# Block products of a gated FFN in another order, with other openings, and VectorE making two low weight parts

## The reference

```python
def swiglu(x, w_gate, w_up, w_down):
    return (jax.nn.silu(x @ w_gate) * (x @ w_up)) @ w_down

x = x + 0.5 * swiglu(rmsnorm(x, ffn1_norm), ffn1_w_gate, ffn1_w_up, ffn1_w_down)
...
x = x + concat([lru_out, ssd_out]) @ w_out
x = x + 0.5 * swiglu(rmsnorm(x, ffn2_norm), ffn2_w_gate, ffn2_w_up, ffn2_w_down)
```

## Time and profile before

| | us |
|---|---|
| median of 3 runs | 2204.09 (2202.66 to 2207.38) |
| the profiled execution, its own time | 2212.14 |
| its span, first to last instruction | 2210.2 |
| TensorE busy | 2140.0 (97%) |
| VectorE, GpSimd, ScalarE busy | 1462.6, 1225.7, 593.7 |
| chain that ended last: TensorE, VectorE, VectorE's queue | 78%, 8%, 4% |

### The profile page before, as it was taken

One profiled execution on the slowest core, in us unless ns is written; L12 is line 12 of the kernel. 1 busy time (PEld: TensorE's weight loads), 2 busy tenths in 40 slices (PEclk: granted clock), 3 DMA queues, 4 the chain that ended last, 5 costly groups with the idle time before them and its releaser, 6 DMA issues.

```text
span 2210.2 us, 36672 instructions
## 1 busy us (share of the span) xinstructions
PE 2140.0 (97%) x15504; PEld 2105.7 (95%) x15504; DVE 1462.6 (66%) x1259; ACT 593.7 (27%) x856; POOL 1225.7 (55%) x825
## 2 busy tenths in 40 slices
PE   6999999988999999899999999999999999989998
PEld 5989999988999999889999999999999999989998
DVE  7797778763222567877888596787888777642215
ACT  5211101111000224577877540122100101110003
POOL 7778888872442322325352663335988888824340
PEclk8999999999999999999999999999999999989999
DMA  4122222226321322311110422132212222363222
GB/s 146 58 77 79 76 77 97 73 101 220 96 73 58 111 93 90 120 65 51 40 60 31 173 87 89 48 116 77 69 67 97 77 77 78 108 221 90 82 58 77
DMA packets 64755, 197.84 MB, mean 90 GB/s; under 512 B 9416, under 2 KB 18120, under 8 KB 64592
## 3 DMA queue, kind: packets, MB, share of 16 engines
q1 hardware_dynamic: 63440, 194.97, 26.0%
q10 hardware_dynamic: 1152, 0.52, 0.1%
HBM read 149.37 MB, written 46.26 MB: 89 GB/s over the span
## 4 chain that ended last, share of the span: by engine, by line
PE 78%; DVE 8%; DVEq 4%; ACT 3%; DMA 2%; issue 2%; POOL 1%; POOLq 1%; ACTq 0%; SPq 0%
PE banks L770 41%; PE banks L850 30%; PE banks L1117 2%; PE banks L815 2%; DMA stage<-hidden 2%; POOLq L663 1%; DVEq L1577 1%; DMA hidden<-up 1%; DVEq L1594 1%; DVE rstd L1538 1%; DVEq L1555 1%; DVE mix L1559 0%; POOL w L664 0%; DVEq L1558 0%; DVE h_lo L1640 0%
## 5 line engine op out<-in xcount | busy, mean ns | idle before, releaser
L623 POOL TENSOR_SCALAR w_hi<-w_raw 128x1024 fp32r<-128x1024 f32 (+1 forms) x93 | 106.6, 1146 | 597.2 <-PE banks L770 531.4
L625 POOL TENSOR_TENSOR w_lo<-w_raw,w_hi 128x1024 fp32r<-128x1024 f32 (+1 forms) x100 | 270.3, 2703 | 162.2 <-DVE xbc L1886 123.4
L770 PE MATMUL banks<-h_hi,w_lo 128*128 128x344 f32 x948 | 306.2, 323 | 14.4 <-DVE x L1672 14.4
L770 PE MATMUL banks<-h_lo,w_hi 128*128 128x344 f32 x948 | 304.9, 322 | 0.0
L770 PE MATMUL banks<-h_hi,w_hi 128*128 128x344 f32 x948 | 304.8, 322 | 0.0
L770 PE MATMUL banks<-u_hi,w_lo 128*128 128x344 f32 x864 | 286.4, 331 | 6.4 <-issue 6.1
L770 PE MATMUL banks<-u_hi,w_hi 128*128 128x344 f32 x864 | 276.4, 320 | 0.0
L770 PE MATMUL banks<-u_lo,w_hi 128*128 128x344 f32 x864 | 276.0, 319 | 0.0
L1672 DVE SCALAR_TENSOR_TENSOR x<-banks,x 128x1032 f32<-128x1032 f32 x42 | 51.7, 1232 | 301.3 <-PE banks L770 301.3
L1197 ACT ACTIVATE parts<-banks 128x516 f32<-128x516 f32 x80 | 47.6, 597 | 659.1 <-PE banks L850 659.1
L770 PEld LDWEIGHTS banks<-h_hi,w_lo 128*128 128x128 f32 x948 | 180.0, 190 | 15.0 <-DVE x L1672 15.0
(11 more groups left out here) (353 smaller groups left out, 5953.4 us busy)
## 6 DMA issues: line engine op xcount, KB each, us to landing
w_raw<-in_gate_up SPq DMA_DIRECT2D x46, 512.0 KB, 4.3
hidden<-up SPq DMA_DIRECT2D x44, 516.0 KB, 6.2
stage<-hidden SPq DMA_DIRECT2D x44, 516.0 KB, 3.6
raw<-in_gate_up SPq DMA_DIRECT2D x40, 512.0 KB, 4.6
w_raw<-in_w_in SPq DMA_DIRECT2D x36, 512.0 KB, 4.2
w_raw<-in_down SPq DMA_DIRECT2D x32, 512.0 KB, 3.9
x<-in_xt SPq DMA_DIRECT2D x16, 516.0 KB, 6.6
x_kept<-x SPq DMA_DIRECT2D x16, 516.0 KB, 5.1
```

The costliest lines, as they stand in the source:

```text
L623: pool.tensor_scalar(w_hi[s][:, 0:n], w_raw[s][:, 0:n], 1.0, 0.0, ALU.mult, ALU.add)
L625: pool.tensor_tensor(w_lo[s][:, 0:n], w_raw[s][:, 0:n], w_hi[s][:, 0:n].bitcast(F32), ALU.subtract).then_inc(split, 1)
L770: end = pe.matmul(out[:, c, 0:CH], w[s][:, k * P:(k + 1) * P], x[kx][:, c * CH:(c + 1) * CH], start=(first and n == 0), stop=(last and n = ...
```

## The change

1. *Order of products.* In a group now p1, p2, p6, p5, p7, p3, p4 (`STEADY`); in group 0 of a block p1, p2, p3, p6, p5, p7, p4 (`OPENING`), whose first two use neither mixes nor weight sums. Only p1 is copied by ScalarE; all others are joined by VectorE straight from PSUM, p7 twice, with one part tile in place of four. The gate or up tile 0 is multiplied by rstd before the join of p4.
2. *Plain units* are three chunks of 344 columns in three banks; copies are one operation each. VectorE reads u1 from PSUM itself, multiplying by rstd, as the last of its four multiplies. Group 0 has new waits: on the root, on that multiply (third product in the first block, second in the second), on the mixes' low parts (fourth). `norm_sum` stands at k = 6.
3. *Opening of the first block.* TensorE runs the high products of g0 and u0 (`highs`), then all low ones (`low`). VectorE makes all low x parts before the mixes, the totals of the norm (GpSimd did), and the low weight parts of g1 and u1 (`low_unit`; GpSimd makes only the high ones, `high_unit`). Three square buffers in place of two, and x4 is squared second.
4. *Second block.* ScalarE takes g0 before the high mixes and u0 before the last of them.
5. *End of a block.* Four stage buffers, of which two are weight buffers freed by group 18. The joins of group 19 come ahead of, and between, the hidden_low operations; ScalarE's hidden_high all follow the last group; the x tiles are loaded in another order, some earlier.
6. *Extras.* `prepare` is cut in four, in groups 1 to 4 of the first block; history and steps move to 5 and 6. z0 is scaled before decode(4).

```diff
+STEADY = ("p1", "p2", "p6", "p5", "p7", "p3", "p4")
+OPENING = ("p1", "p2", "p3", "p6", "p5", "p7", "p4")
+READ = {STEADY: ("p2", "p6", "p5", "p7", "p3", "p4"), OPENING: ("p2", "p6", "p5", "p3", "p7", "p4")}
...
+            f.p = at(f"part{tag}", sums, [HT], skip=3 * 512)
+            f.stage = [at(f"stage{tag}_{n}", tile, [T]) for n, tile in enumerate(stage + raw)]
...
+        f1.g_at, f1.u_at = banks[:, 2:5, 0:CH], banks[:, 5:8, 0:CH]
+        s = AT["os", KT - 1, 0][0]
+        f2.g_at, f2.u_at = (whole_set[:, :, 0:CH] for whole_set in (sets[s], sets[1 - s]))
...
             def load_hidden(f, j):
-                if j >= 2:
-                    sp.wait_ge(*f.hidden.past(j - 1))
-                sp.dma_start(f.stage[j % 2][:], d.hidden[:, j, :]).then_inc(f.stage_landed[j % 2].sem, 16)
+                if j >= 4:
+                    sp.wait_ge(*f.hidden.past(j - 3 if j < 8 else j - 1))
+                n, _ = stage_of(j)
+                sp.dma_start(f.stage[n][:], d.hidden[:, j, :]).then_inc(f.stage_landed[n].sem, 16)
...
                 store_hidden(f, NG // 2 - 1)
+                x_again(f, src, 2)
+                if tag == "2":
+                    x_again(f, src, 7)
+                sp.wait_ge(*f.op_ready.past(7 * (NG - 1)))
+                for j in range(2, 4):
+                    load_hidden(f, j)
...
+                sp.wait_ge(*f.done.past(NOPS))
+                x_again(f, src, 0)
+                x_again(f, src, 1)
+                sp.wait_ge(*f.hidden.past(8))
+                x_again(f, src, 5)
+                x_again(f, src, 6)
+                if tag == "2":
+                    sp.wait_ge(*f.ev.past(6 * NG))
+                    x_again(f, src, 3)
+                    x_again(f, src, 4)
+                store_hidden(f, NG // 2)
                 if tag == "1":
...
+                    x_again(f, src, 3)
+                sp.wait_ge(*f.h_stored.past(32 * (NG // 2 + 1)))
+                if tag == "1":
+                    x_again(f, src, 4)
+                    x_again(f, src, 7)
...
                 tag = f.tag
-                if tag == "1":
-                    for k in range(1, KT):
-                        pool.wait_ge(squared["ffn1"], k + 1)
-                        if k >= 2:
-                            pool.wait_ge(added["ffn1"], k - 1)
-                        pool.tensor_tensor(f.tot[:], f.tot[:], f.c[k % 2][:], ALU.add).then_inc(added["ffn1"], 1)
...
+                    elif o == (1 if f.tag == "1" else 0):
+                        pe.wait_ge(*f.rooted.past(1))
+                    if o == (2 if f.tag == "1" else 1):
+                        pe.wait_ge(*f.taken.past(4))
+                    if o == 3:
+                        pe.wait_ge(*f.mix_lo.past(4))
...
             for k in range(AHEAD):
-                as_it_comes(g, gate, k)
+                highs(g, gate, k)
             for k in range(AHEAD):
-                as_it_comes(u, up, k)
+                highs(u, up, k)
             for k in range(AHEAD, KT):
-                as_it_comes(g, gate, k)
-                as_it_comes(u, up, k)
+                highs(g, gate, k)
+                highs(u, up, k)
+            for k in range(KT):
+                low(g, gate, k)
+            for k in range(KT):
+                low(u, up, k)
...
             def plain_pair(f):
-                dve.wait_ge(*f.taken.past(8))
                 for tile in f.g:
                     last = dve.tensor_tensor(tile[:], tile[:], rstd[:], ALU.mult)
                 last.then_inc(f.scaled.sem, 1)
-                for tile in f.u:
-                    dve.tensor_tensor(tile[:], tile[:], rstd[:], ALU.mult)
+                dve.tensor_tensor(f.u[0][:], f.u[0][:], rstd[:], ALU.mult)
+                dve.wait_ge(used, U(("u" + f.tag, 1)) + 1)
+                dve.tensor_tensor(cut(f.u[1][:]), f.u_at, cut(rstd[:]), ALU.mult).then_inc(f.taken.sem, 1)
                 hidden_pair(f, 0)
...
+                def join(name, a, to, second=None):
+                    o = number(q, name)
+                    dve.wait_ge(*f.done.past(o + 1))
+                    dve.drain()
+                    end = dve.tensor_tensor(halved(to), twos[o % 4], halved(a), ALU.add)
+                    if second:
+                        end = dve.tensor_tensor(halved(second[1]), twos[o % 4], halved(second[0]), ALU.add)
+                    end.then_inc(f.ev.sem, 1)
+                    if between and name in between:
+                        between[name]()
...
+                dve.wait_ge(*f.copied.past(q + 1))
+                join("p2", part, c11)
+                join("p6", part, c21)
+                join("p5", c21, part)
+                if q == 0:
+                    join("p3", part, c12)
+                join("p7", part, c22, (c21, c21))
+                if q:
+                    join("p3", part, c12)
+                dve.drain()
+                if not last:
+                    dve.tensor_tensor(dst[0][:], dst[0][:], rstd[:], ALU.mult)
+                return lambda: join("p4", c21, c21)
...
+                lows = {"p2": lambda: hidden_low(f, 0), "p6": lambda: hidden_low(f, 1),
+                        "p5": lambda: (hidden_low(f, 2), hidden_low(f, 3)), "p7": lambda: hidden_low(f, 4),
+                        "p3": lambda: hidden_low(f, 5)}
...
+            for k in range(2):
+                mixes(f1, k, V_FFN1)
+            low_unit(("g1", 1))
+            for k in range(2, 4):
+                mixes(f1, k, V_FFN1)
+            low_unit(("u1", 1))
+            for k in range(1, KT):
+                dve.wait_ge(squared["ffn1"], k + 1)
+                dve.drain()
+                dve.tensor_tensor(f1.tot[:], f1.tot[:], f1.c[k % 3][:], ALU.add).then_inc(added["ffn1"], 1)
             for k in range(4):
                 mix_low(f1, k)
-            dve.wait_ge(added["ffn1"], KT - 1)
             weight_sums(f1, 0)
             norm_ready(f1)
             plain_pair(f1)
...
+                if q == XT - 1:
+                    decode_scale(5)
+                    scaled(("z", 0), z_early[0][:], rstd)
                 if q >= 7:
                     decode(q - 7)
-            decode_scale(5)
             decode_scale(6)
-            scaled(("z", 0), z_early[0][:], rstd)
             scaled(("z", 1), z_early[1][:], rstd)
```

341 lines of the change are left out of this document (153 added, 188 removed).

## The result

| | before | after |
|---|---|---|
| median of the runs, us | 2204.0 (4 runs, 2202.7 to 2207.4) | 2171.5 (4 runs, 2168.9 to 2172.1) |
| the profiled execution's own time, us | 2212.1 | 2171.1 |
| its span, us | 2210.2 | 2169.4 |

The ratio is 0.9848, 95% interval 0.9831 to 0.9865: 1.5% faster. In two later comparisons the same two kernels gave 0.9812 (0.9797 to 0.9826) and 0.9817 (0.9798 to 0.9836): the changed kernel took 2170.4 and 2170.8 us, the kernel before 2210.4 and 2211.6. So the medians differ by 32.5 us in the table and by 40.0 and 40.8 us later.

What follows compares the result with a forecast made beforehand. TensorE's matmuls, busy 97%, were taken as the bound, with only stalls to win. Gains 4.0 + 7.5 + 16.0 + 1.1 - 4.3 + 16.4 = 40.7 us off the 2204.1 median gave 2163.4, range 2149 to 2182.

Steps and rivals of the forecast that it cites:

- the second group's stall: First block, second group: the wait on ScalarE's copy of p5 and its slow stretch go, gaining 7.5 us.
- z: At the z units: moving only z0 ahead of decode(4) saves one 1.22 us operation; gain 1.1 us, bounds 0 to 3.
- the queue of the first opening: VectorE's work before the third product of group 0, added up to end at 78.4 us, stalling TensorE 14.7 us.
- First opening: First block's start: of 21.7 us of stalls and slow stretches only 4.0 us stay won, because of a new wait.
- Steady groups: Groups after the opening: p2's join is 2.5 us early, the extras eat that; 0 taken, bounds 0 to 6 us.
- Block ends: Last groups and down projection: four buffers and joins ahead of lows gain 16.0 us (10 to 17.4) and 16.4 (8 to 16.4).
- Second opening: Second block's start: 6.2 us gained, a new 7.6 us stall and 2.9 slow lost; net loss 4.3 us (2 to 7).
- Alternation at its worst: Both openings: three SBUF multiplies each wait out a GpSimd instruction, 7.5 us; 4.8 later, 2168.2 us; chance 15%.
- The shorter queue: First opening: VectorE's queue 5.8 us shorter since little of GpSimd's work falls on it; 2154 us; chance 15%.
- the half kept ends: Block ends: half of the stalls stay, from late stage loads and stores queued behind x loads; 16 more, 2180 us; 15%.
- the missed p2 join: Groups behind an up group: p2's join misses its 14.4 us, slower than before; 2224 us at 3 us late each; 4%.
- nothing moves: All stalls: another wait stands right behind each, so nothing is gained; 2204 us; chance 2%.

Runs made afterwards that it cites:

- the run with the low parts ahead: Against the changed kernel, the low parts of the first four hidden tiles are made ahead of the last group's joins in both blocks; 2167.3 us.
- the kernel with four edits: Changed kernel with g1/u1 low weight parts on GpSimd, PSUM up product multiplied first, preparation from group 3 on, second group's weight sums behind the second join; 2158.35 us.
- the up product first: Against the changed kernel, VectorE multiplies the up product out of PSUM first of its four multiplies, not last, in both openings; 2169.0 us.

## Why the prediction was right

**Direction and mechanism.** The places came as forecast: both waits on x_lo gone, the up weights met early, the second group's stall gone, both block ends without a stall over 1 us, and two new stalls, released by VectorE's multiply into up, one at the third product of the first block and one at the second of the second.

**The time.** The predicted 2163.4 is 8.1 below the measured median. The step that failed is the last one, taking the sum off the median of 2204.1 although its terms were read in an execution of 2212.1. Some of those terms were at their long value there (z 6.1 and not 1.4, the down round 5.9 and not 3.6), so they were not all to be had from the median. 2212.1 - 40.7 = 2171.4 would have been the changed kernel's time, and the changed kernel scatters little: 2168.4 to 2172.6 in three comparisons. Beside the later two the medians of before were 2210.4 and 2211.6, and there the sum comes off the median as well (40.0 and 40.8). Why the first median was lower stays open.

That the spans of the two profiles differ by 40.8 us where 40.7 was added up is luck. By the table of stages z gave 4.9 us more than forecast, and the first opening and its groups 5.4 less. The second and third profile of before have spans 34.0 and 35.5 us above the changed kernel's first. In its own adding the prediction has small slips: the queue of the first opening adds up, from its 61.5 on, to 78.1 and not 78.4, the slow stretches behind 528.68 and 933.48 are 2.8 and 1.8 in its sums, as the rows have them, and not 2.9 as its sentence says, and the groups behind an up group are 18 and not 20.

**First opening: 4.0 forecast, about 3.4 got.** The third product started at 79.35 (forecast 78.4) and group 1 at 96.3 (95.7). Inside, errors cancel: VectorE's first subtraction ended at 34.3 and not 31.8, since the gate unit, which it and GpSimd wait for, ended near 31.9 and not at 29.4, and the mixes stood behind that wait; mix_low took 10.89 and not 13.0, the weight sums 4.1 and not 3.1, the three SBUF multiplies 5.10 and not 5.7, the PSUM one 1.22 as forecast. Two things I had at nothing: 1.25 and 1.90 us behind GpSimd's splits of the up weights at 13.38 and 21.22, and 0.86 behind its operand. The gain is 3.4 against the first profile of before, whose group 0 began 2.9 us earlier than the second's and 1.3 later than the third's.

**Steady groups: 0 forecast (bounds 0 to 6), 3.9 measured.** I named the extras of groups 2 and 6 as what would eat the 2.5 us of room and still took 0; groups 2, 4 and 6 stalled (in some profiles only 2 and 6), and with the extras elsewhere none did. It is the low bound of a term whose cause I had in hand.

**Block ends: 16.0 and 16.4 forecast.** The down stages gave 7.8 and 10.9 where their parts of the sum were 7.3 and 11.4 (4.5 and 4.4 for the first against the other two profiles of before); ahead of the down products 0.8 and 0.7 us stayed. By the run with the low parts ahead it was the order of the joins, the single copy or the four buffers, not the place of the lows; which of the three wasn't tried.

**z: 1.1 forecast, 6.0 measured in these two profiles.** Against the second profile of before (527.9 for the stage) the gain is nothing, against the first and third (534.3 and 534.1) it is 6. The wait has two lengths in the kernel before and one in all ten profiles with z0 ahead, though VectorE's two operations were long in each of them. That the move of z0 takes the long wait away is likely by these rows and not shown.

**Second opening: -4.3 forecast, 6.8 - 5.4 - 5.0 = -3.6 got** (5.0 being what the last group's stall gave in the same stage): the stall 7.83 (7.6) and 0.51 of the clock behind it for 4.1 us.

**The rivals.** Alternation at its worst (2168) priced the three multiplies at 7.5 us; they took 5.10 and 4.55. That VectorE is held for whole instructions is nonetheless what the two states at z and the scan show: 1.26 against 3.26, 2.28 against 4.05. The Trainium skill (SBUF — State Buffer, "SBUF: two separate sides") says that whichever of a GpSimd operation and a VectorE one with two SBUF inputs starts first holds the port pair that they share for its whole instruction, and the other is fully blocked. The rows agree at z, where VectorE's long operations began after GpSimd's and end 1.08 or 1.09 us after them; at the scan the starts are too close to tell which was first. The shorter queue (2154) is refuted by the third product at 79.35, the half kept ends (2180) by 0.8 and 0.7, the missed p2 join (2224) by 1.3 us in three groups and nothing in the other 35, "nothing moves" by all rows.

## What to carry over

A stall at an opening names the first wait that TensorE meets, not the bound: add up the other engine's queue to the point where the steady order begins, and judge an edit by when that comes, since freeing one bank only moves the stall to the next. Ahead of a wait on another engine put the work that doesn't need it; a 1.2 us subtraction at the head of a queue held 4.7 us of it idle (the row shows the idle time; no run moved the subtraction). Take a sum that was read in one execution off that execution's time, and profile the kernel before more than once, since some stalls have two lengths in one program.

## What was not expected of the hardware

An elementwise operation of VectorE has two durations in the same place of the same program, by which of it and GpSimd's gets through first: 1.26 or 3.26 us (it began 0.35 us before GpSimd's, or 1.02 after), and a scan 2.28 or 4.05, where the starts are 0.01 us apart in both cases. A stage of the kernel before differs by 6.3 us from this, and one of a variant by 3.4.

Not every stall costs clock: behind 1.9 us TensorE went on at full clock, behind 3.45 it was at half, as the stretches of the kernel with four edits show (stretch, us, busy, granted clock):

```profile
87.30:92.30 5.00, 4.99 (x41) 1.00 0.01 3
1490.30:1495.70 5.40, 5.35 (x25) 0.50 0.52 194
```

Nor does the length of the stall alone decide it. Behind 2.11 us (the kernel with four edits, first down round) the clock was 1.00, behind 2.19 us (the up product first, at 1015.09) 0.62 in the mean of 4 us. And it fell without a stall: behind the same run of short matmuls it stayed at full clock in the changed kernel, the first row, and was at half for some 3 us with the up product first, the second row, which cost 1.5 us:

```profile
808.49:812.49 4.00, 4.00 (x70) 1.00 0.93 240
```

```profile
806.63:810.63 4.00, 4.00 (x62) 0.65 0.93 239
```
